# Stages between mixers and expert loops, taken token tile by token tile

## The reference, cut to what matters

```
x = layer_norm(ALPHA * x + mixer(x));  ALPHA = 4 ** 0.25
scores = sigmoid(x @ router_w);  biased = scores + router_b
top_groups = the best 4 of 8 groups (sum of the two best biased scores)
idx = the best 8 of 64 experts within them;  weights = their scores, normalised, * 2.5
routed = sum of weights * ((silu(x @ w_gate[e]) * (x @ w_up[e])) @ w_down[e])
shared = (silu(x @ sh_gate) * (x @ sh_up)) @ sh_down
x = layer_norm(ALPHA * x + routed + shared)
```

## Time and profile before

| | us |
|---|---|
| median of 3 runs | 1422.64 (1417.32 to 1425.42) |
| the profiled execution | 1420.89 |
| its span, first to last instruction | 1419.1 |
| PE busy | 1351.3 |
| mean granted PE clock | 0.977 |

### The profile page before, as it was taken

The page is one execution under the profiler, slowest core; times in us unless marked ns, Lnnn a source line. Parts: engine busy times, 40 slices in busy tenths (PEclk is TensorE's granted clock), DMA queues, the critical chain, the costliest instruction groups (busy, mean ns, idle before and its releaser), DMA issues.

```text
span 1419.1 us, 17988 instructions
## 1 busy us (share of the span) xinstructions
PE 1351.3 (95%) x6622; PEld 707.0 (50%) x6622; DVE 613.7 (43%) x1197; ACT 344.0 (24%) x690; POOL 50.9 (4%) x95
## 2 busy tenths in 40 slices
PE   6989989999999999999999689999999999999994
PEld 4556546444454444454444565444554444544442
DVE  0766266233434333434434674333434334343336
ACT  1633231222222222222222132222222212222221
POOL 6101010000000000000000200000000000000000
PEclk9999989999999999999999879999999999999997
DMA  9421227699899989998998325999899989989961
GB/s 275 119 85 44 78 95 311 247 388 375 352 410 392 389 345 417 381 388 360 411 390 341 117 89 192 367 388 373 361 409 386 389 364 394 387 345 422 387 278 33
DMA packets 72103, 435.53 MB, mean 307 GB/s; under 512 B 12915, under 2 KB 15075, under 8 KB 22016
## 3 DMA queue, kind: packets, MB, share of 16 engines
q1 hardware_dynamic: 69248, 428.13, 75.8%
q0 software_dynamic: 2816, 6.87, 1.6%
HBM read 433.23 MB, written 1.76 MB: 307 GB/s over the span
## 4 chain that ended last, share of the span: by engine, by line
PE 93%; DVE 5%; ACT 1%; issue 1%; DMA 1%; SPq 0%; DVEq 0%
PE bank L882 32%; PE bank L798 19%; PE bank L830 16%; PE bank L824 13%; PE bank L782 3%; PE bank L1201 3%; PE bank L892 1%; PE bank L989 1%; PE bank L952 1%; PE bank L1280 1%; DVE sb_x L1647 1%; DVE sb_x L1643 1%; DVE sb_ln_st L1639 1%; DMA sb_x<-in_x_sample_dram 1%; DVE sb_att L1749 0%
## 5 line engine op out<-in xcount | busy, mean ns | idle before, releaser
L1576 DVE TENSOR_TENSOR sb_x<-sb_x,bank 128x512 f32<-128x512 f32 (+1 forms) x396 | 242.1, 679 | 118.6 <-PE bank L824 118.6
L830 PE MATMUL bank<-sb_wslot,sb_ht 128*64 128x512 f32 x1024 | 231.0, 593 | 0.0
L882 PE MATMUL bank<-sb_wslot,sb_xg_own 128*64 128x512 f32 x1024 | 226.5, 595 | 1.7 <-ACT sb_xg_own L1332 1.7
L882 PE MATMUL bank<-sb_wslot,sb_xt 128*64 128x512 f32 x1024 | 226.8, 595 | 0.0
L1595 DVE TENSOR_TENSOR sb_hh<-sb_sg,bank 128x256 f32<-128x256 f32 x64 | 27.0, 422 | 375.7 <-ACT sb_sg L1356 375.7
L1582 DVE SCALAR_TENSOR_TENSOR sb_yl<-bank,sb_gslot,sb_yh 128x512 fp32r<-128x512 f32 x128 | 96.1, 751 | 162.6 <-ACT sb_yh L1338 162.6
L798 PE MATMUL bank<-sb_pick,sb_xh 128*128 128x512 f32 x432 | 160.9, 401 | 0.0
L824 PE MATMUL bank<-sb_yh,sb_place 128*128 128x512 f32 x396 | 157.5, 398 | 3.3 <-DVE sb_yl L1582 3.3
L1356 ACT ACTIVATE sb_sg<-bank 128x256 f32<-128x256 f32 x64 | 24.6, 384 | 550.1 <-PE bank L882 550.1
L824 PE MATMUL bank<-sb_yl,sb_place 128*128 128x512 f32 x396 | 156.6, 395 | 0.0
L830 PEld LDWEIGHTS bank<-sb_wslot,sb_ht 128*64 128x64 f32 x1024 | 72.8, 137 | 144.5 <-issue 139.3
(11 more groups left out here) (303 smaller groups left out, 1041.7 us busy)
## 6 DMA issues: line engine op xcount, KB each, us to landing
sb_wslot<-in_moe_w_gate_dram SPq DMA_DIRECT2D x64, 2048.0 KB, 8.3
sb_wslot<-in_moe_w_up_dram SPq DMA_DIRECT2D x64, 2048.0 KB, 13.0
sb_wslot<-in_moe_w_down_dram SPq DMA_DIRECT2D x64, 2048.0 KB, 15.4
sb_w_in_hi<-in_w_in_dram SPq DMA_DIRECT2D x2, 2048.0 KB, 14.5
sb_w_in_lo<-in_w_out_dram SPq DMA_DIRECT2D x1, 4096.0 KB, 12.6
sb_w_in_lo<-in_w_in_dram SPq DMA_DIRECT2D x2, 1024.0 KB, 10.9
sb_ln_g<-in_ln_g_dram POOLq DMA_DIRECT2D x4, 512.0 KB, 4.7
sb_ln_b<-in_ln_b_dram POOLq DMA_DIRECT2D x4, 512.0 KB, 6.0
```

The source lines that it names most:

```text
L830: last = pe.matmul(y_b[c][64 * e:64 * e + 64, :], ht[:, k, 64 * e:64 * e + 64], w_down[u][:, e, k * D + c * 512:k * D + (c + 1) * 512], st ...
L882: last = pe.matmul(gu_b[64 * e:64 * e + 64, :], xgt[b][:, k, sl], w_gu[u][:, :, e, k * FE:(k + 1) * FE], start=k == 0, stop=k == DK_SLICES ...
L1576: dve.tensor_tensor(dst, dst, banks.tile[order[f]][0:rows, :], ALU.add).then_inc(s["added"], 1)
```

## The change

Layer 1 pools tile by tile: band products of tile 0 go to two banks `mx(0, h)`, of tile 1 to `mx(1, h)`. ALPHA x is no longer added by DVE for tiles 0 and 1: PE multiplies x by a diagonal matrix of ALPHA (`residual`, 512 columns a product) into the `po` banks, and the group maps accumulate on top. DVE's statistics and its subtraction read those banks. ACT copies `mx2` only after `ln_sqrt` of tile 0. In both layers PE transposes tile 0, takes its logits and all four shared products of its 128 columns (bank `sh`), and only then transposes tile 1, takes its logits, and so on to tile 2; the shared products of the other 192 columns come as two banks (`sg`, `su`) before `pos`, and none after it. The silu and `gate_hidden` are split the same way. The semaphore `shared_in` becomes two, for gate and up and for down; `silu_ready` is new. GpSimd's memset of the unused columns of `xt` moves from `var_ready` 4 to `x_ready` 6.

The diff, its added lines with their surroundings; the lines that they replace are those printed above.

```diff
+LATER = T_COLS - P
...
+                       ("prev2", 4 * 64), ("alpha", 128)])
...
+    put(band, BAND, "alpha", ALPHA * np.eye(P))
...
     u += [("ogT", t) for t in (1, 2)] + [("mo", 2, c) for c in range(2)]
     for l in range(DEPTH):
         if l:
+            u += [("mx", 0, h) for h in range(2)] + [("po", 0, c) for c in range(2)]
+            u += [("mx", 1, h) for h in range(2)] + [("mx2",)] + [("po", t, c) for t in (1, 2) for c in range(2)]
+        u += [("xT", l + 1, i) for i in range(2)] + [("lgT", l), ("sh", l)]
+        u += [("xT", l + 1, i) for i in range(2, 5)] + [("lg", l), ("sg", l), ("su", l), ("pos", l)]
         u += [("sd", l, t, c) for t in range(TILES) for c in range(2)]
     return u
...
             sp.dma_start(w_rt[:, :, :], a["moe_router_w"][l].rearrange("(p k) e -> p k e", k=8)).then_inc(s["router_in"], 16)
             for name, dst in (("gate", sh_gate), ("up", sh_up), ("down", sh_down)):
                 k = dst.shape[1]
+                sp.dma_start(dst, a[f"moe_sh_{name}"][l].rearrange("(p k) f -> p k f", k=k)).then_inc(s["shared_down_in" if name == "down" else "shared_gu_in"], 16)
         def sp_experts(sp, l):
...
                     for c in range(2):
                         banks.copied(sp, ("po", t, c))
             load_pair(sp, l, 1, 1, GU[1:])
+            banks.full(sp, ("su", l))
             load_pair(sp, l, 1, 1, DN)
             banks.full(sp, ("sd", l, TILES - 1, 1))
             load_pair(sp, l, 1, 1, GU[:1])
...
                     for k in range(2):
                         gp.tensor_tensor(pool_w[:, :, k, :], pool_w[:, :, k, :], pool_s.rearrange("p (g n) -> p g n", g=4), ALU.mult)\
                           .then_inc(s["pool_scaled"], 1)
+                    gp.wait_ge(x_ready, 6)
                     gp.memset(xt[:, :, T_COLS:], 0.0).then_inc(s["init"], 1)
                     gp.dma_start(out["prompt_pool_rows"][0], x[TAIL - 15:TAIL, 2, :]).then_inc(stored, 16)
                     e = SAMPLE_ROW + N_DEC
                     gp.dma_start(out["sample_pool_rows"][0], x[e - 15:e, 2, :]).then_inc(stored, 16)
...
                 if l:
                     pe.wait_ge(s["pool_in"], 16 * 3)
+                    bd = {n: band[:, slice(*BAND[n])].rearrange("p (g t) -> p g t", g=4) for n in BAND if n != "alpha"}
+                    alpha = band[:, slice(*BAND["alpha"])]
+                    def pooled(t):
                         pe.wait_ge(x_ready, 3 + t + 1)
+                        for h in range(2):
+                            ps = banks.open(pe, ("mx", t, h))
+                            for i in range(4):
+                                c = 4 * h + i
+                                g, cc = c // 2, slice(c * P, (c + 1) * P)
+                                last = accumulate(pe, ps[:, i * P:(i + 1) * P], (
+                                    [(x[:, 0, cc], bd["own0"][:, g, :])],
+                                    [(x[:, 0, cc], bd["prev1"][:, g, :]), (x[:, 1, cc], bd["own1"][:, g, :])])[t])
+                            last.then_inc(banks.fill_sem(("mx", t, h)), 1)
+                    def residual(t):
+                        both = [banks.open(pe, ("po", t, c)) for c in range(2)]
+                        for c in range(2):
+                            pe.matmul(both[c][:, :], alpha, x[:, t, c * 512:(c + 1) * 512], start=True, stop=False)
+                        return both
+                    def pooled_part(ps, rows, t, c, g, first):
+                        for k in range(2):
+                            last = pe.matmul(ps[rows, g * PG:(g + 1) * PG], xt[:, 4 * c + 2 * g + k, t * P:t * P + ROWS[t]],
+                                             pool_w[:, 2 * c + g, k, :], start=first and k == 0, stop=k == 1 and (first or g == 1))
+                        return last
+                    def pooled_out(t, both):
+                        for h in range(2):
+                            banks.copied(pe, ("mx", t, h))
+                        for c in range(2):
+                            for g in range(2):
+                                last = pooled_part(both[c], slice(0, P), t, c, g, False)
+                            last.then_inc(banks.fill_sem(("po", t, c)), 1)
+                    pooled(0)
+                    both = residual(0)
+                    pooled(1)
                     pe.wait_ge(s["pool_scaled"], 2)
+                    pooled_out(0, both)
                     pe.wait_ge(x_ready, 6)
                     pe.wait_ge(s["pool_c_in"], 16)
                     ps = banks.open(pe, ("mx2",))
...
                         last = accumulate(pe, ps[:, c * 64:(c + 1) * 64], [
                             (x[:, 1, cc], bd["prev2"][:, g, :]), (x[:, 2, cc], bd["own2"][:, g, :])])
                     last.then_inc(banks.fill_sem(("mx2",)), 1)
+                    both = residual(1)
+                    pooled_out(1, both)
                     banks.copied(pe, ("mx2",))
                     both = [banks.open(pe, ("po", 2, c)) for c in range(2)]
                     for g in range(2):
                         for c in range(2):
+                            last = pooled_part(both[c], second(2, c), 2, c, g, True)
                             if g:
                                 last.then_inc(banks.fill_sem(("po", 2, c)), 1)
+                def shared(ps, c0, name, w, b, cols):
+                    n = cols.stop - cols.start
+                    return accumulate(pe, ps[:, c0:c0 + n], [(w[:, k, b::2], xt[:, k, cols]) for k in range(8)])
+                def logits(t):
+                    cols = slice(t * P, (t + 1) * P)
                     for kk in range(4):
                         for h in range(2):
+                            last = pe.matmul(logit_bank[64 * h:64 * h + 64, cols], w_rt[:, 4 * h + kk, :], xt[:, 4 * h + kk, cols],
                                              start=kk == 0, stop=kk == 3)
                     return last
+                pe_transpose_x(pe, l + 1, (0, 1))
+                pe.wait_ge(s["router_in"], 16)
+                for i in range(2):
                     banks.copied(pe, ("xT", l + 1, i))
+                logit_bank = banks.open(pe, ("lgT", l))
+                logits(0)
+                pe.wait_ge(s["shared_gu_in"], 16 * 2)
+                ps = banks.open(pe, ("sh", l))
+                for b in range(2):
+                    shared(ps, b * P, "sg", sh_gate, b, slice(0, P))
+                for b in range(2):
+                    last = shared(ps, (2 + b) * P, "su", sh_up, b, slice(0, P))
+                last.then_inc(banks.fill_sem(("sh", l)), 1)
+                pe_transpose_x(pe, l + 1, (2, 3))
+                for i in range(2, 4):
+                    banks.copied(pe, ("xT", l + 1, i))
+                logits(1)
                 pe_transpose_x(pe, l + 1, (4,))
                 banks.copied(pe, ("xT", l + 1, 4))
+                pe.wait_ge(s["init"], 1)
+                logits(2).then_inc(banks.fill_sem(("lgT", l)), 1)
                 banks.copied(pe, ("lgT", l))
                 ps = banks.open(pe, ("lg", l))
                 for t in range(TILES):
                     last = pe.matmul(ps[:, t * E:(t + 1) * E], lg_t[:, t * P:(t + 1) * P], const("two_idents"), start=True, stop=True)
                 last.then_inc(banks.fill_sem(("lg", l)), 1)
+                for name, w in (("sg", sh_gate), ("su", sh_up)):
+                    ps = banks.open(pe, (name, l))
+                    for b in range(2):
+                        last = shared(ps, b * LATER, name, w, b, slice(P, T_COLS))
+                    last.then_inc(banks.fill_sem((name, l)), 1)
                 pe.wait_ge(s["sel_ready"], 1)
                 ps = banks.open(pe, ("pos", l))
...
                 accumulate(pe, ps[:, TILES * E:(TILES + 1) * E], [(const("ones"), chosen[:, i, :]) for i in range(TILES)])\
                     .then_inc(banks.fill_sem(("pos", l)), 1)
                 def shared_down():
+                    pe.wait_ge(s["shared_down_in"], 16)
+                    for n in (("sh", l), ("su", l)):
+                        banks.copied(pe, n)
                     token_products("sd", l, lambda k, tc: sh_h[:, k, tc], sh_down, 2)
                 pe_experts(pe, l, shared_down)
...
             for l in range(DEPTH):
                 s = L[l]
                 if l:
+                    for t in range(2):
+                        for h in range(2):
+                            copy(xt[:, 4 * h:4 * h + 4, t * P:(t + 1) * P], ("mx", t, h), lambda ps: ps[:, :].rearrange("p (k n) -> p k n", k=4))
                 def split_high(t):
                     rows = ROWS[t]
...
                     act.activation(xh[0:rows, t, :, :], x[0:rows, t, :].rearrange("p (f k) -> p k f", k=DK_SLICES), ACT.Copy)\
                        .then_inc(s["x_split"], 1)
+                if not l:
                     act.wait_ge(stored, 16 * MIX_STORES)
                 ln_sqrt(2 * l, 0)
+                if l:
```

(28 more changed lines are left out.)

75 lines of the change are left out of this document (1 added, 74 removed).

## The result

The changed kernel takes 1428.36 us (median; 1425.88 to 1431.62) against 1422.66 for the kernel before on the same chip: a ratio of 1.0051, 95% interval 1.0039 to 1.0064. That lies in the range of 1413 to 1432 and 5.4 us above the forecast of 1423.0. It stands on the border of the 0.5% that was called "no change"; the interval shows that it is a small loss. The profiled execution took 1428.75, with a span of 1427.0.

What follows compares the result with a forecast made beforehand. The prediction took PE to bound the kernel (busy 95%, 93% of the chain). Layer 0 -0.1, layer 1 -3.3 and clock falls +5.5 gave +2.1 us on 1420.89, so 1423.0 us, range 1413 to 1432.

Steps and rivals of the forecast that it cites:

- The sums without the clock: Stages before the expert loops, PE at full clock: down product moves -0.1 us in layer 0, -3.3 in layer 1.
- x_ready(3): Layer 0, third token tile normalised: at 209.05 us instead of 204.56, its square root waiting on ACT behind tile 1's copies.
- The load of the round count: PE's load between `pos` and the down product, now exposed: taken at 0.3 us, bounds 0 and 1.1.
- x_ready(7): Layer 1 pooling, first normalisation: at 805.7 us instead of 812.6, the new ACT order removing a stall.
- The statistics from PSUM: Layer 1 pooling, DVE passes reading PSUM: extra cost taken as 0, bounds -0.9 to +0.3 us.
- Eight records of the diagonal: Layer 1 pooling, ALPHA x on PE: 8 records of 0.44 us, 3.5 us of PE work replacing 4 DVE additions.
- the four places: Between logits(1) and logits(2) and before the down product, either layer: PE's clock falls with chance one in two, +5.5 us together.
- The stated price per layer: Cost of PE clock falls: 2.1 us each, 1.3 more after the logits, giving 3.4 there.
- No fall (rival 1): PE's clock does not fall in the four places: -3.4 us, 1417.5 us; chance 0.18.
- Products of tile 0 hidden (2): Tile 0's shared products hidden, as when tile 2's square root is not held up: -11.6 us, 1409; chance 0.13.
- Half clock through the later products (3): PE falls at the logits and stays at half clock through part of the later products: +10.2 us, 1431; chance 0.17.
- The reorder on ACT doing nothing (4): Layer 1: early x_ready(7) gains nothing, PE being late anyway, and the diagonal costs its whole 3.5 us: 1429.8; chance 0.05.

Runs made afterwards that it cites:

- filler: The changed kernel plus products nobody reads, 6 in front of the last logits and 14 behind `pos`, in each layer: ratio 0.9995 to the kernel before, median 1420.79 us.
- pool_only: The changed kernel's pooling of layer 1, with the router stage as in the kernel before: ratio 0.9985 to the kernel before, median 1419.01 us.
- act_order: The changed kernel with ACT's square root of tile 2 and second split ahead of the copies of tile 1: ratio 1.0018 to the kernel before.
- mended_no_fill: The changed kernel with act_order's ACT order, no diagonal, up products in two banks gated before `pos`, no unread products: ratio 0.9991 to the kernel before.
- no_diag: The changed kernel without the diagonal products, DVE adding ALPHA x for all tiles as before: ratio 1.0044 to the kernel before.
- pool_no_diag: pool_only with the ALPHA x additions back on DVE instead of the diagonal products: ratio 0.9982 to the kernel before.
- both_no_diag: both_fixes without the diagonal products, DVE adding ALPHA x: ratio 0.9993 to the kernel before.
- su_half: The changed kernel with one of the four later shared products of each layer moved behind `pos`: ratio 1.0019 to the kernel before.
- both_fixes: The changed kernel with act_order's ACT order and later up products in two banks, one ahead of `pos`, one behind: ratio 0.9996 to the kernel before.
- router_only: The changed kernel's tile-by-tile router in both layers, with the pooling as in the kernel before: ratio 1.0042 to the kernel before.

## Why the prediction was right, and where it fell short

**The sums without the clock held, as far as the marks can tell.** Layer 0 was worked out at -0.1 us and layer 1 at -3.3, at the down product. In filler they are -0.05 and -2.5. Layer 0 of that run is free of falls. Layer 1 isn't: by the fall at 827.40 its last logits begin 1.3 us later behind the transposes than in layer 0 and take 0.3 longer. An estimate without it, from these rows, is -4.1. On the way: x_ready(3) 4.5 late (measured 4.7); routing +4.0 (measured +4.6, of which 0.7 is the product with `two_idents` at half clock, 1.55 for 0.88; the recorded steps themselves add up to 214.9, not 215.1); products of tile 0 7.5 (7.80); from the end of `pos` to the down product 3.7 (3.91 and 3.64). The load of the round count was taken at 0.3, within 0 to 1.1. DVE wrote the count at 235.69, the gate ended at 236.28 and the down product began at 236.90, 0.6 behind the gate where it was 0.1 before: 0.5 exposed.

**Pooling.** The clock was put back at full 11.4 us into the stage, and in the changed kernel it came back at 11.2. x_ready(7) was put at 23.9 us into the stage and came at 25.9: 1.58 of this is a DMA of the layer's norm vector, landing at 811.3, which the old stall on ACT had covered. It cost nothing, since PE's chain was late next, as the prediction said: the transposes start 30.1 us into the stage (worked out 30.9). x_ready(9) was put at 45.0 and came at 44.3. The statistics from PSUM, two passes, took 1.43 us against 1.42 from SBUF: the extra cost taken as 0 was right. The Trainium skill (VectorE: DVE Perf Modes, the TRN2 errata) has a larger fixed part for PSUM; no such difference shows in these rows. Eight records of the diagonal were put at 3.5 us; in pool_only they hold PE for 1.72 and 1.78 us by the starts of what follows. Executions with equally long stretches at half clock in the pooling (6.8 us) show what this costs: PE reaches the first transposes of layer 1 29.0 us into the stage with the diagonal (pool_only, act_order) and 27.0 without it (mended_no_fill), so some 2 us. What is left of that at the end is not settled: no_diag was 1.0 us ahead at the routing of layer 1, pool_no_diag 0.7 ahead at the routing and 0.6 behind at the loop, both_no_diag 3.0 ahead at both. No time separates them.

**The term that was mis-sized is the clock.** The step that failed was "I give each of the four places one in two". All four fell. The row that it rested on spoke for more: the stretches of about 3.5 us do not lie "between 2.4, after which it fell, and nothing", they are longer than the 2.4 us after which the clock fell before. The stated price per layer was 3.4 after the logits and 2.1 at the down product, 5.5 for two of four. From filler to the changed kernel the marks of the down product differ by 2.0 and 1.1 us (an estimated 2.7, if the fall that filler has itself is taken off it), and from there to the gather by 1.5 and 1.6. So each single price was an overestimate, since part of the longer products is covered by the routing, the count was an underestimate, and the sum is 6.3 (or 7.9) against 5.5. The Trainium skill (TensorE: Matmul & The Clock Gate, Part 4) says that transposes do not count like matmuls; by that rule the prediction would have called the falls after the logits near certain, and they did fall. It isn't shown to be the reason: the fillers put products where there was idle time as well as transposes, and a version with idle time filled by transposes wasn't run.

**A step that was missed.** The change opens one PSUM bank fewer in each layer's router stage (`sh`, `sg`, `su` where there were four uses), so all later names shift in the rotation. PE's gather in layer 1 now opens a bank that DVE is still adding from, and waits 0.93. With a full clock the way from the down product to the gather in layer 1 is 9.90 in filler and su_half and 8.90 in the kernel before and both_fixes, which use as many banks as before. So filler's layer 1 ends 1.6 us ahead of before and not 2.5. Together: the marks show +4.7 for the +2.1 of the forecast. Of the 2.6 between them 0.8 lies in layer 1's sum, 0.8 in the falls and 1.0 in this wait.

**What the stages don't explain.** For every changed kernel the measured difference lies 0.8 to 4.9 us above that of its marks: pool_only by 2.5 (-2.1 us by its ratio, -4.6 by marks), both_no_diag by 4.9, the change itself by 2.5 (7.2 by its ratio, 4.7 by marks). So about half of the 5.1 us that the forecast lacks by the ratio lies outside the stages, and its cause stays open. Part of it can be the choice of execution: the profiled one of both_no_diag lies 2.3 us below the median of its runs. The mixer in front of layer 0 ended between 195.0 and 199.6 us in the profiled executions, with the same instructions; in two executions of the kernel before it differs by 2.4 us. Whether the changed programs also shift it on average wasn't separated.

The marks are not firm either. router_only pools with the instructions of the kernel before. The first two rows are of the kernel before, the last two of router_only (a window and the first transposes of layer 1 each):

```profile
783.00:796.60 13.60, 7.84 (x35) 7.58 (x36) 13.04 (x17) 1.75 (x5) 2.78 (x3) 0.50 0.34 140
812.65 1.16 PE L782 MATMUL bank<-sb_cst,sb_x 128*128 128x128 f32 x8
789.40:796.20 6.80, 3.14 (x15) 3.17 (x16) 6.52 (x9) 0.29 (x1) 1.37 (x2) 0.50 0.53 219
815.70 1.16 PE L783 MATMUL bank<-sb_cst,sb_x 128*128 128x128 f32 x8
```

The first transposes come 30.9 us into the stage in one and 28.5 in the other. Differences of layer 1's marks under 2 to 3 us between two single executions therefore show nothing by themselves, nor do times under 0.2%.

**The rivals.** No fall (rival 1): refuted as a forecast; as a sum, filler comes near it (-1.6 us by its marks, -0.7 by its ratio, for -3.4). Products of tile 0 hidden (2): refuted, the square root was held back. Half clock through the later products (3): in its place and with a time 2.6 us from the measured one, half right; all four falls happened, but PE was back at full clock after 6.4 and 10.2 us, and only the part beyond the routing's cover cost. What this nearness in time is worth is open, since 2.5 us of the measured loss lie outside the stages. The reorder on ACT doing nothing (4): in the changed kernel its first half is so, x_ready(7) came 4.2 us before PE reached the transposes; with the old router stage (pool_only) the pooling half is a gain, though no run has ACT's order alone.

One edit that looks natural wasn't tried: moving the square root of tile 0 ahead of the copy of `mx2` in the old pooling order. There the copy also keeps DVE from writing x of tile 1 while PE still reads it, so taking it away alone would be a race.

## What to carry to other kernels

When a step is removed from a PE-bound stage, look at what PE does in the freed time: an idle stretch in front of the next block of products costs twice, once as the wait and once as a slow start, and a few products that nobody reads can be cheaper than the idle. When PE's work is cut into tiles, reorder the in-order queues of the other engines too: here one square root of 0.29 us behind two copies made `x_ready` 3 4.7 us late, and another order on ACT gave 1.9 us of routing back in layer 0. Take such a change apart before judging it: by the ratios one half of this one gained 0.15% and the other lost 0.42%. And look at the granted clock of two traces before comparing their marks: the same instructions differed by 2.4 us with it.
